# First steps of feed-forwards 2 to 4 tile by tile with x stationary; the norms' root and beta moved into the transposition

## The reference

```python
def swiglu(x, w_in, w_out):
    gu = x @ w_in
    g, u = gu[..., :D_FF], gu[..., D_FF:]
    return (jax.nn.silu(g) * u) @ w_out          # D_FF = 2816

for l in range(DEPTH_2):                         # DEPTH_2 = 2
    x = layer_norm_2(ALPHA_2 * x + 0.5 * swiglu(x, ffn_w_in[l, 0], ffn_w_out[l, 0]), ln_g[l, 0], ln_b[l, 0])
    y = mlstm_mixer(...) if l % 2 == 0 else window_attention(...)
    x = layer_norm_2(ALPHA_2 * x + y, ln_g[l, 1], ln_b[l, 1])
    x = layer_norm_2(ALPHA_2 * x + 0.5 * swiglu(x, ffn_w_in[l, 1], ffn_w_out[l, 1]), ln_g[l, 2], ln_b[l, 2])

def layer_norm_2(x, g, b):
    mu = mean(x); var = mean((x - mu) ** 2)
    return (x - mu) * rsqrt(var + LN_EPS) * g + b
```

## Time and profile before

| | |
|---|---|
| median of three runs | 1694.35 us (1694.08 to 1695.98) |
| profiled execution | 1697.26 us, span 1695.5 us, mean granted TensorE clock 0.976 |
| TensorE matmul busy | 1592.3 us, 94% |
| VectorE, ScalarE, GpSimd busy | 779.7 us (46%), 505.8 us (30%), 61.4 us (4%) |
| chain that ended last | PE 67%, DMA 14%, DVE 10% |
| DMA | mean 233 GB/s over the span |

### The profile page before, as it was taken

One profiled execution on the slowest core, in us unless ns is written; L12 is line 12 of the kernel. 1 busy time (PEld: TensorE's weight loads), 2 busy tenths in 40 slices (PEclk: granted clock), 3 DMA queues, 4 the chain that ended last, 5 costly groups with the idle time before them and its releaser, 6 DMA issues.

```text
span 1695.5 us, 21971 instructions
## 1 busy us (share of the span) xinstructions
PE 1592.3 (94%) x9238; PEld 1172.1 (69%) x9238; DVE 779.7 (46%) x1028; ACT 505.8 (30%) x573; POOL 61.4 (4%) x104
## 2 busy tenths in 40 slices
PE   8997899999999998999998899999999997899997
PEld 7744433333333336999896689998999986689997
DVE  1584411111111116544656675456544566564445
ACT  1251100000000003334354234342443435433432
POOL 2000000000000000000000000000000000000000
PEclk9997899999999999999999999999999998999999
DMA  6705799999999999753223578554554221387500
GB/s 198 250 1 232 290 415 429 428 429 429 428 428 429 429 412 353 268 183 114 75 78 122 174 243 292 185 185 161 202 190 157 98 76 74 100 288 264 193 0 26
DMA packets 149457, 395.27 MB, mean 233 GB/s; under 512 B 9442, under 2 KB 109920, under 8 KB 136592
## 3 DMA queue, kind: packets, MB, share of 16 engines
q1 hardware_dynamic: 146656, 385.67, 60.5%
q0 software_dynamic: 2736, 8.68, 1.4%
HBM read 393.28 MB, written 1.05 MB: 233 GB/s over the span
## 4 chain that ended last, share of the span: by engine, by line
PE 67%; DMA 14%; DVE 10%; issue 3%; SPq 3%; ACT 2%; POOL 1%; POOLq 0%; DVEq 0%; ACTq 0%
PE bank L1355 29%; DMA ring<-in_moe_w_dram 14%; PE bank L1368 12%; PE bank L885 8%; PE bank L914 2%; PE bank L697 2%; SPq L267 2%; PE bank L1343 2%; PE bank L1575 1%; PE bank L902 1%; PE bank L644 1%; PE bank L1900 1%; PE bank L934 1%; DVE stats L539 1%; PE bank L683 1%
## 5 line engine op out<-in xcount | busy, mean ns | idle before, releaser
L885 PE MATMUL bank<-ring,arena 128*64 128x512 f32 x928 | 228.4, 596 | 9.5 <-DMA ring<-in_moe_w_dram 9.5
L1355 PE MATMUL bank<-x_hi,split_u_hi 128*128 128x256 f32 x688 | 194.9, 283 | 0.0
L1355 PE MATMUL bank<-x_hi,split_u_lo 128*128 128x256 f32 x688 | 194.7, 283 | 0.0
L1355 PE MATMUL bank<-x_lo,split_u_hi 128*128 128x256 f32 x688 | 194.7, 283 | 0.0
L1355 PE MATMUL bank<-x_lo,split_g_hi 128*128 128x256 f32 x656 | 185.6, 283 | 0.0
L1355 PE MATMUL bank<-x_hi,split_g_lo 128*128 128x256 f32 x656 | 185.6, 283 | 0.0
L1355 PE MATMUL bank<-x_hi,split_g_hi 128*128 128x256 f32 x656 | 185.6, 283 | 0.0
L885 PEld LDWEIGHTS bank<-ring,arena 128*64 128x64 f32 x928 | 69.3, 137 | 146.3 <-issue 114.7
L1265 DVE TENSOR_TENSOR split_g_lo<-ring,split_g_hi 128x2048 fp32r<-128x2048 f32 x47 | 107.7, 2292 | 127.7 <-ACT split_g_hi L1259 127.7
L1115 DVE SCALAR_TENSOR_TENSOR arena<-arena,work 128x256 f32<-128x256 f32 x32 | 15.5, 485 | 287.7 <-PE bank L934 287.7
L1265 DVE TENSOR_TENSOR split_u_lo<-ring,split_u_hi 128x2048 fp32r<-128x2048 f32 x45 | 103.1, 2292 | 69.0 <-ACT split_u_hi L1259 69.0
(11 more groups left out here) (352 smaller groups left out, 2504.8 us busy)
## 6 DMA issues: line engine op xcount, KB each, us to landing
ring<-in_moe_w_dram SPq DMA_DIRECT2D x92, 2048.0 KB, 19.1
ring<-in_ffn_w_in_dram SPq DMA_DIRECT2D x88, 1024.0 KB, 5.5
ring<-in_ffn_w_out_dram SPq DMA_DIRECT2D x44, 1024.0 KB, 5.5
ring<-in_ml_w_in_dram SPq DMA_DIRECT2D x12, 1024.0 KB, 5.2
ring<-in_rec_w_in_dram SPq DMA_DIRECT2D x10, 1024.0 KB, 11.6
ring<-in_at_w_in_dram SPq DMA_DIRECT2D x6, 1024.0 KB, 5.2
ring<-in_rec_w_out_dram SPq DMA_DIRECT2D x5, 1024.0 KB, 13.6
gb_row<-in_ln_g_dram POOLq DMA_DIRECT2D x8, 512.0 KB, 7.3
```

Of the source, the lines that this page charges most:

```text
L885: i = nc.tensor.matmul(bank[4 + p][64 * j:64 * j + 64, :], xe[p][:, k, :], unit_view(n, 4)[:, k % 4, :], start=(k == 0), stop=(k == KT - 1))
L1355: i = nc.tensor.matmul(up_bank(kind, s_)[:, m * T:(m + 1) * T], w, xp_[b][:, k, :], start=(k == 0 and j == 0), stop=(k == KT - 1 and j == 2))
```

## The change

For the norms 1 to 6 (`SPLIT_NORMS`) VectorE ends with `centred`. ScalarE makes `turn_diag`, the identity scaled by the root of each token, and TensorE multiplies `x_tok` by it, a float32 matmul, where it had transposed. Ahead of that it puts beta into the bank, a matmul of `beta_r` (high and low part on partitions 0 to 3 and 32 to 35) by `blocks_r`, a pattern of ones; the transposition adds to it. `x_tok` itself is completed later, in `finish_rows`: within step 0 of the feed-forwards, or after two weight splits in the mixers. Beta is loaded a second time for it by GpSimd, copied by ScalarE and its low part formed by VectorE at each such norm.

For f = 1 to 3 the first step has x stationary, one tile after the other: 128 tokens come out on the partitions, 256 hidden features along them, gate and up together. The order is transposition of tile 0, high x of tile 0 by both weight parts, transposition of tile 1, the same of tile 1, then the low x of each. There is no warming there. The up weights of this step stay in the ring, in their own slot and the next one, which gets an empty unit; they are split ahead of the norm. h of this step has tokens on the partitions, and TensorE transposes it into bank 4 after `up(0, 1)`. ScalarE's order in step 0 is silu, gate split, up split, h, down split.

Some semaphores and small buffers are merged or moved for room, and the two constants `beta` and `blocks_r` are set up by VectorE in the mixture of experts; these edits are left out below.

```diff
+NORM_AHEAD, NORM_AFTER = (1, 3, 4, 6), (2, 4, 5, 7)
 
...
-                units.append((k, src, (f_lo[kind], NSTEP * f + s_ + 1)))
+                if f > 0 and (kind, s_) == (1, 0):
+                    units.append((k, src, (f_mm[1], NSTEP * f + 1)))
+                    units.append((0, None, (f_mm[1], NSTEP * f + 1)))
+                else:
+                    units.append((k, src, (f_lo[kind], NSTEP * f + s_ + 1)))
...
+            if L in SPLIT_NORMS:
+                parts = bs.rearrange("o (b k p) -> (o k) b p", b=2, p=P)
+                pool.wait_ge(G["ln_blo"], 2)
+                for row in (0, 32):
+                    pool.dma_start(beta[row:row + 4], parts).then_inc(s_gbrow, 16)
...
+        def finish_rows(dve, L):
+
+            for t in range(TT):
+                for hf in range(2):
+                    dve.wait_ge(G["ln_tr"], 4 * L + 2 * t + hf + 1)
+                    scaled_rows(dve, L, t, hf)
...
+            if L in SPLIT_NORMS:
+                dve.wait_ge(s_gbrow, rows_loaded(L))
+                dve.wait_ge(G["ln_bhi"], SPLIT_NORMS.index(L) + 1)
+                nc.vector.tensor_tensor(beta_r[32:36], beta[32:36], beta_r[32:36].bitcast(F32), ALU.subtract).then_inc(G["ln_blo"], 1)
+                for t in range(TT):
+                    residual(t, 0)
+                    residual(t, 1)
+                    moments(t)
+                    centred(t, 0)
+                    centred(t, 1)
...
+            if L in SPLIT_NORMS:
+                act.wait_ge(s_gbrow, rows_loaded(L))
+                act.wait_ge(G["ln_tr"], 4 * L)
+                nc.scalar.activation(beta_r[:], beta[:], ACT.Copy).then_inc(G["ln_bhi"], 1)
             for t in range(TT):
+                if L in SPLIT_NORMS:
+                    act.wait_ge(G["ln_rstd"], 2 * L + t + 1)
+                    nc.scalar.activation(turn_diag[:, t, :], ident[:], ACT.Copy, scale=rstd[:, t:t + 1]).then_inc(G["ln_diag"], 1)
...
-        def norm_pe(pe, L):
-            for t in range(TT):
-                keep_warm(pe, WARM[t])
+        def norm_pe(pe, L, tiles=range(TT), warm=None):
+            for t in [tiles] if isinstance(tiles, int) else tiles:
+                keep_warm(pe, WARM[t] if warm is None else warm)
+                n = SPLIT_NORMS.index(L) if L in SPLIT_NORMS else None
+                if n is not None:
+                    pe.wait_ge(G["ln_blo"], n + 3)
+                    pe.wait_ge(G["ln_cen"], 4 * n + 2 * t + 1)
+                    for b in range(2):
+                        nc.tensor.matmul(bank[4 + 2 * t + b][:], beta_r[:, b, :], blocks_r[:], start=True, stop=False,
+                                         skip_group_check=True)
+                    pe.wait_ge(G["ln_diag"], 2 * n + t + 1)
...
-                        pe.wait_ge(G["ln_half"], 4 * L + 2 * t + k // 4 + 1)
-                    i = nc.tensor.transpose(bank[4 + 2 * t + k // 4][:, (k % 4) * P:(k % 4 + 1) * P],
-                                            x_tok[:, t, k * P:(k + 1) * P], ident[:])
+                        if n is None:
+                            pe.wait_ge(G["ln_half"], 4 * L + 2 * t + k // 4 + 1)
+                        else:
+                            pe.wait_ge(G["ln_cen"], 4 * n + 2 * t + k // 4 + 1)
+                    o = bank[4 + 2 * t + k // 4][:, (k % 4) * P:(k % 4 + 1) * P]
+                    if n is None:
+                        i = nc.tensor.transpose(o, x_tok[:, t, k * P:(k + 1) * P], ident[:])
+                    else:
+                        i = nc.tensor.matmul(o, x_tok[:, t, k * P:(k + 1) * P], turn_diag[:, t, :], start=False, stop=(k % 4 == 3),
+                                             skip_group_check=True)
...
-            return slots(f)[0 if kind == 2 and s_ == NSTEP - 1 else kind]
+            if f > 0 and (kind, s_) == (1, 0):
+                n = at_unit["f", f, 1, 0]
+                return ring_r[:, (n + 1) % RING, :], ring_r[:, n % RING, :]
+            return [part[:] for part in slots(f)[0 if kind == 2 and s_ == NSTEP - 1 else kind]]
...
+            elif f > 0 and (kind, s_) == (1, 1):
+                act.wait_ge(G["ln_in"], 4 * (NORM_AFTER[f - 1] + 1))
             elif s_ > 0:
                 act.wait_ge(f_mm[kind], NSTEP * f + s_)
-            elif f > 0 and kind > 0:
+            elif f > 0 and kind == 2:
                 act.wait_ge(G["ln_in"], 4 * (NORM_AFTER[f - 1] + 1))
-            elif f > 0:
+            elif f > 0 and kind == 0:
                 act.wait_ge(f_mm[1], NSTEP * f)
...
+            if f > 0 and (kind, s_) == (1, 0):
+                here(act, n + 1)
...
-            split_act(act, f, 1, 0)
+            if f == 0:
+                split_act(act, f, 1, 0)
...
+                if by_tile:
+                    split_act(act, f, 1, 1)
+                    act.wait_ge(f_turn, f)
+                    nc.scalar.activation(h_hi[:, 0], h_turned, ACT.Copy).then_inc(f_hhi, 1)
+                    split_act(act, f, 2, 0)
+                else:
+                    act.wait_ge(f_h, c + 1)
+                    nc.scalar.activation(h_hi[:, s_ % 2], h_raw, ACT.Copy).then_inc(f_hhi, 1)
+                    if s_ < NSTEP - 1:
+                        split_act(act, f, 1, s_ + 1)
+                        split_act(act, f, 2, s_)
+                if f == 1 and s_ == NSTEP - 2:
+                    split_act(act, 2, 1, 0)
...
+            if f == 0:
+                split_dve(dve, f, 1, 0)
...
+                if by_tile:
+                    split_dve(dve, f, 1, 1)
...
+                if by_tile:
+                    nc.vector.tensor_tensor(h_lo[:, 0], h_turned, h_hi[:, 0].bitcast(F32), ALU.subtract).then_inc(f_hlo, 1)
+                    split_dve(dve, f, 2, 0)
...
+                if f == 1 and s_ == NSTEP - 2:
+                    split_dve(dve, 2, 1, 0)
+                if s_ == 0:
+                    finish_rows(dve, NORM_AHEAD[f])
...
+        h_turned = bank[4][:].rearrange("p (m t) -> p m t", m=2)
+
+        def norm_and_ffn_pe(pe, f, L):
+            n_split = SPLIT_NORMS.index(L)
+
+            def first_of_tile(t, part):
+                x = xp_[part]
+                for k in range(KT):
+                    if k % 4 == 0:
+                        if part == 0:
+                            pe.wait_ge(G["ln_evac"], 4 * L + 2 * t + k // 4 + 1)
+                        else:
+                            pe.wait_ge(G["ln_lo"], 4 * n_split + 2 * (k // 4) + t + 1)
+                    for kind in range(2):
+                        for n, w in enumerate(place_of(f, kind, 0)[0:2 - part]):
+                            i = nc.tensor.matmul(bank[kind][:, t * FSTEP:(t + 1) * FSTEP], x[:, k, t * P:(t + 1) * P],
+                                                 w[:, k * FSTEP:(k + 1) * FSTEP],
+                                                 start=(t == 0 and part == 0 and k == 0 and n == 0),
+                                                 stop=(part == 1 and k == KT - 1), skip_group_check=True)
+                        if part == 1 and t == 1 and k == KT - 1:
+                            i.then_inc(f_mm[kind], 1)
+
+            norm_pe(pe, L, 0)
+            pe.wait_ge(f_lo[0], NSTEP * f + 1)
+            pe.wait_ge(f_lo[1], NSTEP * f + 1)
+            first_of_tile(0, 0)
+            norm_pe(pe, L, 1, 0)
+            first_of_tile(1, 0)
+            first_of_tile(0, 1)
+            first_of_tile(1, 1)
+            ffn_pe(pe, f, L)
...
-            up_first()
-            up(1, 0, base)
+            if f == 0:
+                up_first()
+                up(1, 0, base)
             for s_ in (1, 2):
                 up(0, s_, base + s_)
+                if f > 0 and s_ == 1:
+                    pe.wait_ge(f_h, base + 1)
+                    for m in range(2):
+                        for t in range(TT):
+                            i = nc.tensor.transpose(h_turned[:, m, t * P:(t + 1) * P], h_raw[:, t, m * P:(m + 1) * P], ident[:])
+                    i.then_inc(f_turn, 1)
...
-            norm_pe(pe, 3)
-            ffn_pe(pe, 1, 3)
-            norm_pe(pe, 4)
-            ffn_pe(pe, 2, 4)
+            norm_and_ffn_pe(pe, 1, 3)
+            norm_and_ffn_pe(pe, 2, 4)
             norm_pe(pe, 5)
             at_pe(pe)
-            norm_pe(pe, 6)
-            ffn_pe(pe, 3, 6)
+            norm_and_ffn_pe(pe, 3, 6)
...
+            split_act(act, 1, 1, 0)
...
+            split_act(act, 3, 1, 0)
...
+            split_dve(dve, 1, 1, 0)
...
+            split_dve(dve, 3, 1, 0)
```

More of the change, by code:

```diff
@@ L127, in build @@
         ident = sb("ident", [P, P])
+        small_at = nc.sbuf_base
+        MS = sb("ml_small", [P, 256])
+        raw_at = nc.sbuf_base
+        misc_raw = sb("misc_raw", [8 * CH, P])
+        ng_raw = sb("ng_raw", [KT, P])
+        beta = nc.alloc_sbuf_tensor_at("beta", [36, 2, P], F32, offset=raw_at)
+        iota_at = nc.sbuf_base
+        iota_s = sb("iota_s", [P, SLOTS])
+        blocks_r = nc.alloc_sbuf_tensor_at("blocks_r", [36, HALF], F32R, offset=iota_at)
```

(44 more changed lines are left out.)

139 lines of the change are left out of this document (68 added, 71 removed).

## The result

The changed kernel takes 1717.04 us (median of 4 runs, 1716.16 to 1717.85) against 1694.21 us (4 runs, 1694.04 to 1695.98): ratio 1.0133, 95% interval 1.0119 to 1.0146. It is 22.8 us slower (20.2 to 24.7 by that interval), where +16.0 was forecast; the time lies on the upper edge of the range, 1717. The profiled execution took 1716.16 us with a span of 1714.5, granted clock 0.970 (before: 1697.26, 1695.5, 0.976).

What follows compares the result with a forecast made beforehand. TensorE, busy 94% of the span, was taken as the bound. Terms 14.6 + 5.2 + 1.3 (turning h) - 5.8 + 0.4 + 0.3 = +16.0 us on the median 1694.35 gave 1710 us, range 1701 to 1717.

Steps and rivals of the forecast that it cites:

- stall per feed-forward, with its tail: Before step 1 of feed-forwards 1 to 3, TensorE waits 4.86 us for the gate weights' split: +14.6 us.
- E to the first step's end: E is when TensorE finishes the last projection before the norm; the first step's matmuls end 16.4 us later.
- boundary, three together: Norms 3, 4 and 6 to the first step's end get shorter by 1.1, 1.65 and 3.05, together -5.8 us.
- clock behind the stalls: Lower clock behind each of three TensorE stalls loses 1.7 us of work, +5.2 us; ends 0 and 2.5 each.
- norms 2, 5: TensorE is the later engine and reaches the first step later: +0.2 us each, bounds -0.8 and +1.
- norm 1: Tile 0 starts 1.4 us later on VectorE, slow clock doubles new matmuls: +0.3 us, bounds -1.7 and +3.
- mixers, rest of feed-forward 0: No cost: finish_rows adds 2.9 us to VectorE's queue where it idles; without that cover up to 2.9 us each.
- (c): Faster, 1690.5 us: the split of gate step 1 overlaps the first step, stall below 1.2 us; chance 0.06.
- (d): Next to no change, 1694 us: half of the stall is covered and the clock stays up; chance 0.03.
- (a): The stall before step 1 comes without the clock loss behind it: 1705 us; chance 0.18.
- The fp32 transposition: At each boundary, matmuls in place of real transposes take 2.4 of the 16.4 us to the first step's end.
- (b): VectorE falls behind too: finish_rows makes gate step 2 late, clock loss 2.5 each: 1715 to 1716 us; chance 0.11.

Runs made afterwards that it cites:

- kernel with the turned order: Changed kernel with the up projection of step 1 ahead of its gate projection, up's weight splits earlier, in feed-forwards 2 to 4: 1695.33 us, ratio 1.0001.
- the filling: Changed kernel with 16 warming matmuls in front of step 1's first projection in feed-forwards 2 to 4: 1709.55 us, against 1717.59 us for the changed kernel beside it.
- the kernel with the norms alone: Changed kernel without the tile-by-tile first step: norms 1 to 6 keep root and beta in the transposition, feed-forwards as before: 1700.04 us, ratio 1.0027.
- the tiled versions with and without a real transpose: Changed kernel with step 1's up projection ahead of its gate projection: 1685.35 us with plain transposes in all norms, 1695.33 us with the matmul transposition.
- the kernel with the tiles alone: Changed kernel with plain transposes in all norms, first step of feed-forwards 2 to 4 still tile by tile: 1708.42 us, ratio 1.0085.

## Why the prediction was right in kind and short in size

| step | forecast | measured |
|---|---|---|
| stall per feed-forward, with its tail | 4.86 | 4.86 (4.70 + 0.16) |
| E to the first step's end | 16.4 | 16.86 |
| boundary, three together | -5.8 | -4.4 |
| clock behind the stalls, up to the next norm or the end | +5.2 | +5.6 |
| turning h | +1.3 | +1.1 (0.36 each) |
| norms 2, 5 | +0.4 | +1.1 |
| norm 1 | +0.3 | +1.6 |
| mixers, rest of feed-forward 0 | 0 | +1.4 |

With the three stalls (14.6) the measured terms add up to 21.0; the rows of the first table without its first one give 21.1 (rounding).

**The stall.** Its cause, place and length are right: a chain that used to run under the up projection of step 0 has lost its cover because both projections of step 0 end together. The kernel with the turned order shows it by the cure. Rivals (c) and (d) fall: the wait is 4.70 us, not under 1.2. The split can be covered, but by step 1's other projection, not by the first step.

**The clock.** The mechanism is shown by the filling, and rival (a) falls with it. The size is near: half of the 12.0 us at 0.50 is 6.0. The changed kernel against the one with the turned order gives 1.43, 1.97 and 2.24 behind the three restarts, 5.6 together, and another 0.7 in the attention mixer; the filling gives back 5.3. The Trainium skill (TensorE: Matmul & The Clock Gate, HAM oscillation — how this bites in real kernels) counts the penalty as the throttled time times one half; by it these rows give 6.0, and the traces agree within 0.4 and 0.7. The attention mixer further on has the same waits in both traces (14.4 us in 4), yet a mean clock of 0.93 before and 0.90 after. That the stalls do this isn't shown. With plain transposes the clock there is 0.90 behind stalls and 0.93 without or with filled ones; but the kernel with the norms alone, which has no such stall, has 0.90 as well, and the one with the turned order 0.93:

```profile
1380.58:1497.04 116.46, 97.59 (x631) 82.28 (x631) 73.34 (x123) 53.17 (x124) 4.35 (x6) 0.90 0.24 82
1375.93:1491.66 115.73, 96.83 (x631) 81.58 (x630) 74.95 (x124) 55.23 (x125) 4.35 (x6) 0.93 0.21 73
```

**The boundary** is the first term that failed. I gave a tile's transposition with its two beta matmuls 2.37 us; it takes 2.60 for tile 0 (988.36 to 990.96) and 2.50 for tile 1, and the 32 matmuls between them take 3.98 where 3.8 was reckoned. The spacing inside a run of equal matmuls doesn't show what a change from one kind to the next adds, here 0.1 to 0.2 us each time. Over three boundaries 1.4 us.

**The fp32 transposition.** The prediction put 2.4 of the 16.4 us on it. With plain transposes the step ends at 14.34: 2.52. That the two are close is chance, for the 2.4 doesn't follow from the rows: for two tiles they give 2.1 us for the matmuls alone (1.92 less 0.87 each) and 3.0 with the beta matmuls (0.45 each). The run has the 3.0, less two waits of 0.34 and 0.18 or 0.20 that TensorE still has with plain transposes. It is a loss once TensorE is the late one. The Trainium skill (Perfetto Trace Analysis, Transposes) wants a real transpose here, and by that rule all six norms lose; the tiled versions with and without a real transpose (1685.35 and 1695.33) agree, though with the norms' half alone norm 6 became 0.83 shorter: there the old form had waited for VectorE and then lost 1.7 us to the clock.

**Norms 1, 2 and 5** are the second term that failed: 2.7 us against 0.7. At norms 2 and 5 I had E+6.7; it is E+6.93, by the same hand-overs, and before it was not the E+6.45 of norm 4 but 6.42 and 6.30. At norm 1 I had tile 0 coming 1.4 us later through VectorE; TensorE's wait for it is only 0.24 longer (4.82 against 4.58), and the delay is TensorE's own. The rows after:

```profile
648.07 1.19 PE L672 MATMUL bank<-blocks_r,beta_r 36*128 36x512 f32 x2 [4.82 <-DVE x_tok L583]
649.19 3.78 PE L685 MATMUL bank<-turn_diag,x_tok 128*128 128x128 f32 x16
```

At half clock the two take 4.7 us, where the 8 transposes of tile 0 took 1.5. The gain behind them came as foretold: 12 of the first step's first matmuls in 1.69 us, full clock, against 3.77 us for 16. So the first step starts 2.7 us later after the last MoE matmuls, not 1.7. How much of this stays goes with where the low clock falls: with the same norm 1 the row of the first table is +1.6 here and +1.7 in two other traces, +0.9 with the turned order and +0.1 with the filling; in the five traces with the old norm 1 it is the same to 0.04.

**The mixers** are the third, put at nothing. Of the 1.4 us 0.9 are in the attention mixer (109.5 against 108.7), 0.5 in the other mixer and feed-forward 0. It isn't a fixed price of the change either: with the turned order and the same norms the three come to 0.3.

**The cover of gate step 2**, rival (b): foretold with 1.1 us to spare.

```profile
1022.53 2.73 DVE L557 SCALAR_TENSOR_TENSOR x_tok<-x_tok,rstd,gb_row 128x512 f32<-128x512 f32 x4
1025.18 2.29 DVE L1348 TENSOR_TENSOR split_g_lo<-ring,split_g_hi 128x2048 fp32r<-128x2048 f32 x1
```

That split ends at 1027.5, and TensorE takes it up at 1028.90 without a wait: 1.4 to spare. The 22.8 us resemble the price of (b) (21 to 22) but have nothing to do with it. To the 16.0 come five terms (boundary, clock, norm 1, norms 2 and 5, mixers) that were each 0.4 to 1.4 too low, together 5.2, less 0.2 for turning h, and the 1.7 that stay open.

**The range** holds the time by luck. Its top, 1717, was meant for (b), which did not happen, and the sums behind both ends are off: (b) with norm 1 high gives 1718 to 1719, and the low end, 1705 less 2.0 and 3.1, gives 1700 and not 1701.

## What to carry to other kernels

When two projections that used to follow each other are made to end together, ask whose split, copy or load used to run under the second one; here the change was 22 us slower by that alone, and issuing the two projections of the next step the other way round made it break even. A wait of TensorE that can't be removed can be filled with matmuls on data at hand: the wait stays, its clock loss goes. In three kernels here that was worth 5.3, 9.3 and 6.2 us by the traces (8.0, 9.2 and 5.9 by the medians). Where low phases fall differs between traces even where the code is the same, so a difference of 1 or 2 us at such a place needs more than one trace. Shortening the tail of an engine by giving TensorE dearer work only pays where that engine stays the late one afterwards; here it was shorter at norm 6 alone, and that by a clock fall that it avoided.

## What the runs showed that was not expected

Stalls of one length did not cost one amount of clock: behind stalls of 4.70, 4.69 and 4.70 us the clock stayed at 0.50 for 2.96, 4.33 and 4.72 us, and in the kernel with the tiles alone, behind stalls of the same length, for up to 6.2. Filling all but 1.12 us of the stall kept it at 1.00 every time. The new matmul form of the transposition, 8 for one tile, took 1.9 us at full clock and 3.6 at half, so before a norm that begins in a cold phase it costs twice.
